# Skewing the first mixer's token tiles around its norms, and moving small work off TensorE's way

## The reference

```python
z = h @ w_in                       # q, k, v, o (512 each), gates (16), gu, gv (512 each)
qk = silu(depthwise_conv(concat(q, k)) + conv_b)
h_fwd = mlstm_chunkwise(qh, kh, vh, i_f, f_f); h_bwd = ...   # gates give i and f, per token and head
x = x + parallel_mixer(rms_norm(x, g_mix), ...)              # ends in "@ w_out"
x = x + memory_cross_attention(rms_norm(x, g_xattn), rms_norm(mem, g_mem), w_q_x, w_kv_x, w_o_x)
x = x + hier_moe(rms_norm(x, g_moe), ...)   # top-1 of 4 groups, top-2 of its 8 experts, 32 experts of width 512
```

## Time and profile before

| what | us |
|---|---|
| runs of the kernel before, median (lowest, highest) | 1897.16 (1896.32, 1899.91) |
| the profiled execution, its own time | 1899.93 |
| span of that execution, first to last instruction | 1898.1 |
| TensorE busy | 1709.6 |
| VectorE busy | 466.7 |
| ScalarE busy | 255.8 |

### The profile page before, as it was taken

How to read it: one execution, slowest core, us unless ns; L and a number is a source line. 1 busy time by engine, 2 the same in 40 slices (tenths; PEclk the granted TensorE clock), 3 DMA queues, 4 the chain that set the end, 5 groups by cost and what they waited for, 6 DMA issues and landing times.

```text
span 1898.1 us, 18662 instructions
## 1 busy us (share of the span) xinstructions
PE 1709.6 (90%) x8120; PEld 1163.8 (61%) x8120; DVE 466.7 (25%) x984; ACT 255.8 (13%) x560; POOL 23.9 (1%) x45
## 2 busy tenths in 40 slices
PE   8999997766666876699999999999999999999998
PEld 7466574321222322387688868884786788698853
DVE  3314113301112211232512222220334321232211
ACT  2222121000000000113211011110113210011000
POOL 0001000000000000000000000000000000000000
PEclk9999997987989988799999999999999999999999
DMA  8432453899999999933314433345343134343160
GB/s 325 150 136 79 198 235 133 342 430 429 430 430 430 430 430 430 384 146 133 111 67 158 169 139 133 134 157 195 133 177 130 48 133 156 133 178 145 77 243 22
DMA packets 31696, 405.16 MB, mean 213 GB/s; under 512 B 3520, under 2 KB 3840, under 8 KB 7168
## 3 DMA queue, kind: packets, MB, share of 16 engines
q1 hardware_dynamic: 31040, 400.96, 52.8%
q10 hardware_dynamic: 576, 3.01, 0.4%
HBM read 402.92 MB, written 1.05 MB: 213 GB/s over the span
## 4 chain that ended last, share of the span: by engine, by line
PE 79%; DMA 18%; DVE 2%; issue 1%; ACT 1%; POOL 0%; DVEq 0%; SPq 0%; ACTq 0%; POOLq 0%
PE bank L1044 77%; DMA zone<-in_w_experts 10%; DMA w<-in_w_experts 7%; PE bank L1088 1%; DMA x<-in_x 0%; POOL stat L2769 0%; ACT zone L1463 0%; DVE zone L1871 0%; DVE zone L2093 0%; ACT zone L1445 0%; DVE zone L1631 0%; DVE zone L1645 0%; ACT zone L1454 0%; DVE zone L2108 0%; DVE zone L2045 0%
## 5 line engine op out<-in xcount | busy, mean ns | idle before, releaser
L1044 PE MATMUL bank<-zone,w 128*128 128x256 f32 (+1 forms) x4096 | 814.0, 361 | 3.4 <-DVE zone L1645 2.4
L1044 PEld LDWEIGHTS bank<-zone,w 128*128 128x128 f32 x4096 | 722.8, 192 | 95.6 <-issue 5.6
L1044 PE MATMUL bank<-w,zone 128*128 128x512 f32 (+1 forms) x1760 | 521.8, 649 | 70.0 <-DMA w<-in_w_experts 60.3
L1044 PEld LDWEIGHTS bank<-w,zone 128*128 128x128 f32 (+1 forms) x1760 | 203.8, 157 | 364.9 <-issue 288.2
L1044 PE MATMUL bank<-zone 128*32 128x512 f32 (+10 forms) x1928 | 330.6, 493 | 72.5 <-DMA zone<-in_w_experts 48.9
L1044 PEld LDWEIGHTS bank<-zone 128*128 128x128 f32 (+2 forms) x1928 | 193.6, 172 | 212.7 <-issue 132.7
L1463 ACT ACTIVATE zone<-bank 128x512 f32<-128x512 f32 (+1 forms) x128 | 72.4, 574 | 755.9 <-PE bank L1044 568.5
L2562 DVE TENSOR_SCALAR zone<-zone,vec 128x256 f32<-128x256 f32 x68 | 28.1, 413 | 256.8 <-ACT zone L2419 256.8
L1088 PE MATMUL bank<-const,zone 128*128 128x128 f32 (+2 forms) x286 | 43.3, 295 | 27.6 <-DVE zone L1631 12.9
L2419 ACT ACTIVATE zone<-bank 128x256 f32<-128x256 f32 x68 | 24.9, 384 | 320.7 <-PE bank L1044 320.7
L1088 PEld LDWEIGHTS bank<-const,zone 128*128 128x128 f32 (+2 forms) x286 | 35.3, 152 | 42.1 <-issue 15.4
(11 more groups left out here) (233 smaller groups left out, 497.1 us busy)
## 6 DMA issues: line engine op xcount, KB each, us to landing
w<-in_w_layers SPq DMA_DIRECT2D x68, 2048.0 KB, 8.0
w<-in_w_experts SPq DMA_DIRECT2D x52, 2048.0 KB, 27.5
zone<-in_w_experts SPq DMA_DIRECT2D x47, 2048.0 KB, 27.5
w<-in_w_first SPq DMA_DIRECT2D x16, 2048.0 KB, 8.0
w<-in_w_layers SPq DMA_DIRECT2D x6, 1024.0 KB, 5.1
zone<-in_row ACTq DMA_DIRECT2D x2, 1024.0 KB, 5.4
zone<-in_table SPq DMA_DIRECT2D x1, 1664.0 KB, 17.7
zone<-in_table SPq DMA_DIRECT2D x1, 1216.0 KB, 15.8
```

The lines of the kernel that those rows point to most:

```text
L1044: return eng.matmul(out, lhsT, rhs, start=start, stop=stop, **kw_)
```

## The change

- *Weights*: `vx1` moves in the list of slots from behind `vx0` to behind `qx1`. SyncE issues `small1` behind slot 0 and `row1` behind slots 1 and 2. The gate weights in `small1` are padded to 32 columns.
- *Skew*: `q` and `qx0` become `tall_by_tiles`: both halves of the slot for tile 0 with the transposes of tile 1 between them, then both for tile 1. In `out` and `xo` (`widest`) tile 0's transposes of the next norm are issued ahead of the last two products. `route` is one product for each tile.
- *Gates*: eight products with the gate weights stationary, on four column groups, evacuated by ScalarE and folded by `gtok`, behind `k`.
- *Order*: `kx1` from ahead of `gcol` to ahead of `st`; `vx0` from there to ahead of `ny`; `vx1` from there to behind `sc`. The row exponentials from behind the `kx1` copies to between `gu` and `gv` on ScalarE, `Rn` accordingly on VectorE.
- *Norms*: ScalarE squares in halves of 512, each after its addition; VectorE adds, scales and evacuates tile by tile.
- *Routing*: `choose` and `weigh` for each tile; five `rank` products, three of which need tile 0 alone; some work moved ahead, three steps fused or dropped.
- *Passes*: TensorE waits for `Pe` ahead of `in`, for `Pw` ahead of its transposes, and for `in1` only from the third slot.
- `widest` and `early` are shared with the layers, whose order of work stays as it was.

```diff
 PE
-            norm_T(pl, "nx", hs, sem("hs"), 2)
-            for evacuated in banks.taken_up(pl, *[f"nx{g}" for g in range(4)]):
+            norm_tile_T(pl, "nx", hs, sem("hs"), 1, 0)
+            for evacuated in banks.taken_up(pl, "nx0", "nx1"):
                 eng.wait_ge(*evacuated)
+            tall_by_tiles(pl, "q", hT, "nx", 2)
             eng.wait_ge(*pl.need(sem("ld_small1"), 16))
-            group(pl, "gates", [((P, 16 * t, 16), [(hT[:, c, t * P:(t + 1) * P], small1[:, 16 * c:16 * c + 16])
-                                                    for c in range(KT)]) for t in range(TT)])
-            tall(pl, "q", hT, 4)
+            bank = opened(pl, "gates")
+            for c in range(KT):
+                o = c % 4 * 32
+                ins = mm(bank[o:o + 32, 0:T], small1[:, 32 * c:32 * c + 32], hT[:, c, :], c < 4, c >= 4)
...
             tall(pl, "k", hT, 4)
+            group(pl, "gtok", [((P, CAP * t, CAP), [(gpart[:, t * P:(t + 1) * P], cv("fold"))]) for t in range(TT)])
...
+        def early(pl, name, w, cols, act, t, last=False):
+            bank = banks.tile(pl, name) if last else opened(pl, name)
+            for j in range(2):
+                summed(pl, bank[:, j * T + t * P:j * T + (t + 1) * P],
+                       [(w[j][:, k * 512 + cols[j]:k * 512 + cols[j] + P], act[:, k, t * P:(t + 1) * P]) for k in range(KT)],
+                       name if last and j == 1 else None)
+        def tall_by_tiles(pl, pre, act, norm, n):
+            k, w = slot(pl)
+            for g in range(2):
+                early(pl, f"{pre}{g}", (w, w), (2 * g * P, (2 * g + 1) * P), act, 0)
+                if g == 0:
+                    norm_tile_T(pl, norm, hs, sem("hs"), n, 1)
+            for evacuated in banks.taken_up(pl, f"{norm}2", f"{norm}3"):
+                eng.wait_ge(*evacuated)
+            for g in range(2):
+                early(pl, f"{pre}{g}", (w, w), (2 * g * P, (2 * g + 1) * P), act, 1, True)
+            release(k)
...
         def widest(pl, pre, act, norm, n_hs, ready=None):
...
+                        if (n, t, c) == (1, 1, 6):
+                            norm_tile_T(pl, norm, hs, sem("hs"), n_hs, 0)
...
+            for evacuated in banks.taken_up(pl, f"{norm}0", f"{norm}1"):
+                eng.wait_ge(*evacuated)
...
-            widest(pl, "out", hT)
-            norm_T(pl, "nq", hs, sem("hs"), 6)
-            tall(pl, "qx0", hT, 4)
+            widest(pl, "out", hT, "nq", 5)
+            tall_by_tiles(pl, "qx0", hT, "nq", 6)
             tall(pl, "qx1", hT, 4)
...
+            widest(pl, "xo", oT, "ne", 7)
+            for t in range(TT):
+                if t == 1:
+                    norm_tile_T(pl, "ne", hs, sem("hs"), 8, 1)
...
+                group(pl, f"route{t}", [((P, 0, 36), [(hT[:, c, t * P:(t + 1) * P], small1[:, 768 + 36 * c:804 + 36 * c])
...
+            for i, (at, t, m) in enumerate(((0, 0, up_to), (1, 0, every), (2, 0, every), (1, 1, up_to), (2, 1, every))):
+                eng.wait_ge(*pl.need(sem("assigned"), t + 1))
 ACT
+        def squares_after(pl, pre, norm, gain):
+            for n in range(2):
+                square_after(pl, pre, n, 0)
+            square_after(pl, pre, 0, 1)
+            evac_T(pl, norm, hT, None, gain, [0])
+            square_after(pl, pre, 1, 1)
+            evac_T(pl, norm, hT, None, gain, [1])
 DVE
-            add_and_scale(pl, "out", 6)
-            evac_T(pl, "nq", hT, None, "g_xattn")
+            for t in range(TT):
+                add_and_scale(pl, "out", 4, t)
+                evac_T(pl, "nq", hT, None, "g_xattn", [t])
...
+            for t in range(TT):
+                add_and_scale(pl, "xo", 8, t)
+                evac_T(pl, "ne", hT, None, "g_moe", [t])
+            for t in range(TT):
+                choose(pl, t)
+                if t == 0:
+                    weigh(pl, t)
+            weigh(pl, 1)
 SP
-            eng.dma_start(small1, dram["w_small1"]).then_inc(*pl.up(sem("ld_small1"), 16))
-            eng.dma_start(row1, dram["row1"]).then_inc(*pl.up(sem("ld_row1"), 16))
             weights(0, 1)
+            eng.dma_start(small1, dram["w_small1"]).then_inc(*pl.up(sem("ld_small1"), 16))
             eng.dma_start(const[:, P:], dram["const"][:, P:]).then_inc(*pl.up(sem("ld_const"), 16))
             weights(1, 3)
+            eng.dma_start(row1, dram["row1"]).then_inc(*pl.up(sem("ld_row1"), 16))
```

More of the change, by code:

```diff
@@ L50 @@
 FIRST_SLOTS = [("q", SLOT), ("k", SLOT), ("v", SLOT), ("gu", SLOT), ("gv", SLOT), ("o", SLOT),
-               ("kx0", SLOT), ("kx1", SLOT), ("vx0", SLOT), ("vx1", SLOT),
-               ("out0", SLOT), ("out1", SLOT), ("qx0", SLOT), ("qx1", SLOT), ("ox0", SLOT), ("ox1", SLOT)]
+               ("kx0", SLOT), ("kx1", SLOT), ("vx0", SLOT),
+               ("out0", SLOT), ("out1", SLOT), ("qx0", SLOT), ("qx1", SLOT), ("vx1", SLOT), ("ox0", SLOT), ("ox1", SLOT)]
 ESLOTS = 12
@@ L972, in program @@
     row1 = z.take(ROW1["all"][1])
-    small1 = z.take(128 + 512 + 288)
+    small1 = z.take(256 + 512 + 288)
     after_first = z.at
@@ L1190, in first @@
                 transposes(pl, f"kt{t}", [(P, h * P, P, qk[:, 4 + h, t * P:(t + 1) * P], ident) for h in range(H)])
-            wide(pl, "vx0", hmT)
+            tall(pl, "kx1", hmT, 4)
             for hp in range(2):
@@ L1218, in first @@
                                              for j in range(2)])
-            wide(pl, "vx1", hmT)
+            wide(pl, "vx0", hmT)
             norm_T(pl, "ny", y, sem("y"), 2)
@@ L1378, in extra @@
                 ins.then_inc(*xbanks.close(pl, kind))
-            for kind, part in (("gate", gpart), ("up", upart)):
+            for kind, part in (("gate", gsum4), ("up", upart)):
                 for evacuated in xbanks.taken_up(pl, kind):
@@ L1520, in first @@
                 A(ev, ev, ACT.Exp, scale=-1.0).then_inc(*pl.up(sem("Eexp")))
-            for t in range(TT):
-                copy(pl, f"vx0{t}", vx[:, t, 0:512])
+            for g in range(2):
+                copy(pl, f"kx1{g}", kx[:, 4 + 2 * g:6 + 2 * g, :].rearrange("p c t -> p (c t)"))
             for r in range(2):
@@ L1534, in first @@
             for t in range(TT):
-                copy(pl, f"vx1{t}", vx[:, t, 512:1024])
+                copy(pl, f"vx0{t}", vx[:, t, 0:512])
             evac_T(pl, "ny", hT)
-            square_sum_after(pl, "out")
-            evac_T(pl, "nq", hT, None, "g_xattn")
+            squares_after(pl, "out", "nq", "g_xattn")
             for i in range(2):
@@ L1670, in first @@
             evac_T(pl, "nx", hT, None, "g_mix")
-            eng.wait_ge(*banks.filled_up(pl, "gates"))
-            bank = banks.tile(pl, "gates")
-            eng.wait_ge(*pl.need(sem("ld_row1"), 16))
-            for t in range(TT):
-                ins = V.tensor_tensor(gtok[:, t, :], bank[:, 16 * t:16 * t + 16], rv(ROW1, row1, "gate_b"), ALU.add)
-                if t == 0:
-                    ins.then_inc(*pl.up(vstep))
-            ins.then_inc(*banks.done(pl, "gates"))
             def conv(c):
@@ L1698, in first @@
                 conv(c)
+            eng.wait_ge(*banks.filled_up(pl, "gtok"))
+            bank = banks.tile(pl, "gtok")
+            eng.wait_ge(*pl.need(sem("ld_row1"), 16))
+            for t in range(TT):
+                ins = V.tensor_tensor(gtok[:, t, :], bank[:, CAP * t:CAP * t + 16], rv(ROW1, row1, "gate_b"), ALU.add)
+                if t == 0:
+                    ins.then_inc(*pl.up(vstep))
+            ins.then_inc(*banks.done(pl, "gtok"))
             eng.wait_ge(*banks.filled_up(pl, "rowi"))
@@ L2859, in expert_pass @@
             weights(5, 6, 7, 8)
-            eng.wait_ge(*banks.filled_up(before, "route"))
+            eng.wait_ge(*banks.filled_up(before, "route1"))
             weights(9, 10, 11)
```

307 lines of the change are left out of this document (147 added, 160 removed).

## The result

The changed kernel takes **1872.44 us** (median of 4, 1871.34 to 1877.62) against 1896.76 us (1896.32 to 1899.91) for the kernel before, a ratio of 0.9874 [0.9852, 0.9895]. Measured again later with a fresh set of runs of both: 1874.43 against 1897.41, 0.9885 [0.9869, 0.9901]. So 23 to 24 us are won where 21.3 were forecast. The profiled executions are 28.4 us apart (1899.93 and 1871.56, spans 1898.1 and 1869.4); the last part of the experiments comes back to that gap.

A forecast was written before the change was run, and what follows sets the result against it. TensorE up to pass 0 (333.12 us) sets the time, with a fixed-length stream of expert weight transfers behind it. Seven terms sum to 21.3 us: 1878.6 from the profiled 1899.93, 1876 us off the median, range 1867 to 1886.

The forecast's parts named there:

- Step 1: Start to `v`: `q` starts on tile 0 with weights at 11.5 us, gates shrink; `v` 5.0 us earlier (2 to 6.5).
- Step 2: Ahead of `gcol`: row exponentials and reversal move behind `gu`, removing TensorE's idle time; 3.9 us (3.5 to 3.9).
- Step 3: `gcol` to `kt`: without the idle time the clock may stay up; half of 4.9 taken, 2.6 us (0.5 to 4.9).
- Step 4: `out` to `sc`: norm skewed by tiles, less a 2.9 us stall and 2.0 for the clock; 1.5 us (0.5 to 6).
- Step 5: Softmax between `sc` and `ox`: `vx1` covers the gap, transposes remain; 2.1 us (1.5 to 2.3).
- Step 6: `xo` to pass 0's `in`: routing by tiles, VectorE setting the pace after a 2.9 us stall; 5.2 us (4 to 8).
- Step 7: `in` to the first gate product: the wait for `in1` goes; 1.0 us (0.8 to 1.3).
- Rival A: Hand-overs behind `out` and `xo`: no stall and the clock holds, so 32 us gained, 1865 us; chance 0.1.
- B: Start gives little: slot 0 lands late, clock falls at every narrow stretch; 15 us gained, 1882 us; chance 0.17.
- C: Half-width products in `q` and `qx0` are slow, 0.213 us a record, costing 26 us: 1902 us; chance 0.03.
- D: Stream of transfers alone sets the end, the stall before pass 1 grows by the gain: no move, 1897 us; chance 0.05.

The follow-up runs named there:

- twice: Changed kernel with the 32 records of `vx1` issued once more before the real ones: 1886.86 us, ratio 0.9945 to the kernel before.
- q_whole: Changed kernel with `q` taken back to whole 256-column products behind the transposes of both tiles: 1870.12 us, ratio 0.9854 to the kernel before.
- norms_whole: Changed kernel with the norms behind `out` and `xo` taken back to both tiles and `qx0` whole, routing by tiles kept: 1875.82 us.
- add_first: Changed kernel with VectorE adding half 0 of tile 1 before evacuating tile 0's transposes, in `out` and `xo`: 1871.56 us.

## Why the prediction held

The forecast was 1876 us within 1867 to 1886, faster. The time is 1872.4, and the mechanism was the one predicted: all of the gain lies on TensorE ahead of pass 0, and `twice` shows that such a shift passes to the end undiminished. The chain, however, is not equally well read at every step, and a part of the good fit is luck: for an execution like the profiled one the forecast was 1878.6 us and 1871.56 were measured, 7.0 less. The median lies only 3.6 us below its forecast because the other executions of the changed kernel were slower, which the prediction did not consider.

- **Step 1, start.** 4.8 for 5.0, by partly other terms. The weights landed at 12.05, not 11.5; the clock's slow part of `q` cost 1.5 us more than full rate instead of 2; the gates took 1.07 us for 0.9. The gates gave 5.4 (6.82 from start to start, now 1.37 with `gtok`; read from the two timelines, not undone in a run); `q` and `k` cost 0.9 more by the transposes and half widths; 0.3 is the earlier start of `q`, which holds the 3.0 of the queue's order, as without it the weights come at 15.04. The skew of `q` is worth -1.4: the sum counted its transposes, but did not ask when `q` could start without it. With both tiles transposed that was 11.99, just when the weights land.
- **Step 2.** 3.8 for 3.9, and the idle 3.86 come back exactly when undone.
- **Step 3, clock behind the rows.** Half of 4.9 was taken, 3.3 measured. The clock did fall without an idle gap before it, in every profile in which the gap was gone. The premise that transposes, as in `gcol`, are no activity for the clock does not fit `q_whole`, where it rose at 10.5 us and TensorE had run nothing but transposes, from 7.67 us on; and the 0.51 ahead of `route`, taken as agreement, stood behind idle gaps of 2.4 and 1.0 us as well. What in `gcol` and `mu` let it fall stays open. The granted clock in `mu` and `sp` reads:

```profile
116.60:119.80 3.20, 3.20 (x16) 2.68 (x15) 2.34 (x10) 1.69 (x2) 0.21 (x1) 1.00 0.95 307
120.20:123.00 2.80, 2.80 (x17) 2.80 (x18) 2.72 (x11) 1.55 (x3) 2.80 (x5) 0.62 0.85 357
```

- **Step 4, `out` to `sc`.** This is the mis-sized term: 1.5 forecast, 5.0 measured, and both halves of the error have a place. The idle time was put at 2.9 us, as 3.7 of hand-over less 0.86 of products behind the transposes. But the transposes stand ahead of the last two products, which are four records and 1.88 us (190.64), and the hand-over took 3.3: 1.45. The second is the 2.0 us deducted for a falling clock. It stayed up:

```profile
193.90:197.60 3.70, 3.63 (x32) 3.63 (x33) 0.97 (x2) 0.63 (x3) 0.56 (x1) 1.00 0.58 168
```

1.5 + 1.4 + 2.0 = 4.9. With the norm whole, 3.4 us idle in two pieces, it fell again for 6.8 us. The bound of 6 covered it.
- **Step 5.** 2.6 for 2.1, above its bound of 2.3: the transposes ahead of `ox` took 1.75 us from start to start, not 2.0, and 0.16 is the tail of `sc`, over which the next group now starts. Undone, 2.6 return.
- **Step 6, `xo` to `in`.** 7.6 for 5.2. `choose(0)` was to start 7.0 to 8.9 us after the end of `xo` and did so at 288.32, 6.3 after, mostly by the same shorter stall. From there VectorE's chain was 10.2 us for the 10.8 added up. VectorE's first routing instruction, before and after:

```profile
313.35 0.12 DVE L1880 MEMSET zone<- 128x80 f32 x1 [7.19 <-PE bank L1044]
...
288.32 0.15 DVE L1964 TENSOR_TENSOR zone<-bank,zone 128x4 f32<-128x4 f32 x1
```

It came 40.4 us after the start of `xo` before and 34.9 after, and the chain to `in` went from 12.3 to 10.2 us: 5.5 and 2.1 make the 7.6. The skew of the norm alone is 1.1 of the 5.5 (`norms_whole`). That the rest is the routing by tiles fits both timelines, but no run undoes it.
- **Step 7.** 1.9 for 1.0: 1.12 of the wait, which came back to the hundredth, and the rest the clock in `in` (5.38 us for 6.13).

Rival A (1865) was half right: the stall exists, but it is half as long and the clock held. B fell with the start. C fell with 96 records of 128 columns in 10.88 us, 0.113 each. The Trainium skill's sustained 81 ns for a matmul of 128 columns (TensorE: Matmul & The Clock Gate, "Back-to-back issue gap"), from which the estimate of 0.16 us a record came, is not borne out for these records. D fell with `twice`.

The terms add up to 27 to 29 us in the profiles and the medians say 23 or 24. Part of that is shown: the start of `q` and the clock (1.9 us at the gate between two profiles of one kernel) and the expert passes (3 us). That executions without a profile lean to the long side of both for this kernel and not for the kernel before is inferred from their times; no trace of one exists.

## What to carry to other kernels

Find the point behind which the kernel is a fixed length, here within 3 us, and double one known group ahead of it to prove it; after that every microsecond can be counted in one engine's timeline. When a tile is skewed around a norm, look at what the first tile waits for on its own: if that is a weight transfer, as at `q`, the skew costs its split products and hides nothing. At a hand-over, count the idle time twice, once as the gap and once as the half clock that may follow it (3.86 us idle ahead of `gcol` cost 2.6 to 4.2 more, 1.45 behind `out` nothing more), and put the next tile's small work ahead of the current tile's evacuation on the shared engine.

## What the runs showed of the hardware

- The clock's first rise is not fixed by the program. With `q` starting at 12 to 15 us it came at 10.5 to 19.4 us of the span in the profiles of the changed kernel and its edits, at 15.1 and 16.9 in two executions of the same one. At 10.5 us, in `q_whole`, TensorE had run only transposes. In the kernel before it came at 23.3 both times. Ahead of it the trace records no granted clock; the rate tells it: eight transposes took 1.94 us at 7.62 and 1.04 us at 17.14.
- The clock fell at 116 to 122 us of the span in all profiles without the gap, with no idle time before it, 2.4 to 5.3 us after the start of `gcol`; `gcol` and `mu` use 4 rows of the array. It fell within `mu`, or, as in the first profile, 0.9 us into the products behind it (120.9 us), or in the wide products that stood between two parts of `mu`. It came back after 3.4 us or after 6.8, in two executions of one kernel once each.
- An idle gap of 1.45 us behind `out` left the clock at 1.00 until 284.7 us. Behind `xo`, where narrow products and transposes follow, the same gap was followed by half clock from 284.7 us; with the gap ahead of `route0` removed (`add_first`) it fell all the same, at 286.2.
- Sixteen f32 records of 256 columns on four column groups took 1.07 us, 0.067 each, a little over the 0.056 that their 512-column kin suggest.
- The expert passes, bound by transfers at 429 GB/s, varied by 3 us from one execution to the next (461.2 to 464.0 over fourteen profiles).
